# Two-block transformer kernel on one core: the RWKV projections in another order, with a third of the weight splits on GpSimd

## The reference, cut to what matters

```python
x = x + rmsnorm(e, g[5])                    # end of PLE
h = rms_norm(x, g_mix[layer])
h_prev = jnp.pad(h, ((0, 0), (1, 0), (0, 0)))[:, :-1]
hh = h_prev - h
xr, xw, xk, xv, xa, xg = (h + hh * mu[i] for i in range(6))
r = xr @ w_r
w = -softplus(-(w0 + tanh(xw @ w1) @ w2)) - 0.5
k = xk @ w_k
v = xv @ w_v
a = sigmoid(a0 + (xa @ a1) @ a2)
g = sigmoid(xg @ g1) @ g2
kk = k * k_k ; kk = kk / max(norm(kk per head), 1e-12)
k = k * (1 + (a - 1) * k_a)
decay = exp(-exp(w))
# then, for each token: state = state * decay + (state @ -kk) (kk * a)^T + v k^T ; y = state @ r
y = groupnorm(y) + sum(r * k * r_k) * v
x = x + (y * g) @ w_o
```

## Time and profile before

| | |
|---|---|
| median of 3 runs | 1519.14 us (1517.55 to 1521.77) |
| the profiled execution's own time | 1517.85 us |
| its span from first to last instruction | 1516.1 us |
| busy: PE, DVE, ACT, POOL | 94%, 61%, 48%, 10% of the span |
| granted TensorE clock, mean | 0.967 of full speed |
| memory read | 228.51 MB, 151 GB/s over the span |
| PE busy from 678.0 to 821.6 us, the stretch that is changed | 123.31 us of 143.60 |
| DVE, ACT, POOL busy in the same stretch | 114.55, 71.95, 19.80 us |

### The profile page before, as it was taken

How to read it: one execution, slowest core, us unless ns; L and a number is a source line. 1 busy time by engine, 2 the same in 40 slices (tenths; PEclk the granted TensorE clock), 3 DMA queues, 4 the chain that set the end, 5 groups by cost and what they waited for, 6 DMA issues and landing times.

```text
span 1516.1 us, 25989 instructions
## 1 busy us (share of the span) xinstructions
PE 1418.1 (94%) x10670; PEld 1214.2 (80%) x10670; DVE 918.8 (61%) x1257; ACT 724.5 (48%) x976; POOL 147.3 (10%) x138
## 2 busy tenths in 40 slices
PE   8988999998999999988889988899999988799998
PEld 8956888987988999876767766799998865589997
DVE  5665555556576645578877585655555665355563
ACT  5454545446545554454653343354444665254452
POOL 0162011100000110100030011000000123000000
PEclk9999999999999999998998999999999999799999
DMA  8733465564654556544453000365474631245562
GB/s 285 239 92 124 149 207 175 175 192 155 212 165 158 188 188 221 182 154 118 143 177 98 5 3 3 105 216 181 143 244 129 224 110 56 82 163 184 160 214 86
DMA packets 82262, 231.27 MB, mean 153 GB/s; under 512 B 11696, under 2 KB 17472, under 8 KB 82144
## 3 DMA queue, kind: packets, MB, share of 16 engines
q1 hardware_dynamic: 81584, 227.49, 47.0%
q0 software_dynamic: 560, 2.11, 0.4%
HBM read 228.51 MB, written 1.06 MB: 151 GB/s over the span
## 4 chain that ended last, share of the span: by engine, by line
PE 83%; DVE 7%; ACT 4%; issue 3%; POOL 2%; DMA 1%; SPq 0%; DVEq 0%; ACTq 0%; POOLq 0%
PE PS L410 51%; PE PS L413 28%; PE PS L425 4%; ACT SH L382 1%; DVE SL L385 1%; POOL AB L771 1%; DVE XI L1284 1%; DVE AB L745 1%; DVE SL L388 1%; DMA ST<-in_w_attn_in 0%; POOL SM L839 0%; ACT AB L755 0%; DVE LG L1572 0%; DMA ST<-in_w_conv_in 0%; DVE MG L1581 0%
## 5 line engine op out<-in xcount | busy, mean ns | idle before, releaser
L388 DVE SCALAR_TENSOR_TENSOR SL<-ST,SM,SH 128x1024 fp32r<-128x1024 f32 (+1 forms) x256 | 314.8, 1249 | 179.8 <-ACT SH L382 138.5
L382 ACT ACTIVATE SH<-ST,SM 128x1024 fp32r<-128x1024 f32 (+1 forms) x256 | 282.3, 1122 | 215.1 <-PE PS L413 137.9
L410 PE MATMUL PS<-XH,SH 128*128 128x256 f32 x1256 | 353.2, 281 | 5.2 <-DVE XL L1289 3.3
L413 PE MATMUL PS<-XH,SL 128*128 128x256 f32 x1256 | 353.4, 281 | 0.0
L410 PE MATMUL PS<-XL,SH 128*128 128x256 f32 x1256 | 352.4, 281 | 0.0
L385 DVE TENSOR_TENSOR SL<-ST,SH 128x1024 fp32r<-128x1024 f32 (+1 forms) x167 | 216.9, 1315 | 155.1 <-ACT SH L382 131.3
L410 PE MATMUL PS<-SH,XH 128*128 128x512 f32 x576 | 241.3, 419 | 24.0 <-DVE XL L1773 7.5
L382 ACT ACTIVATE SH<-ST 128x1024 fp32r<-128x1024 f32 (+1 forms) x167 | 172.1, 1047 | 181.2 <-PE PS L413 150.4
L410 PEld LDWEIGHTS PS<-XH,SH 128*128 128x128 f32 x1256 | 237.4, 189 | 6.9 <-ACT SH L382 5.7
L410 PEld LDWEIGHTS PS<-XL,SH 128*128 128x128 f32 x1256 | 235.1, 187 | 1.0
L413 PEld LDWEIGHTS PS<-XH,SL 128*128 128x128 f32 x1256 | 235.2, 187 | 0.2
(11 more groups left out here) (310 smaller groups left out, 1433.3 us busy)
## 6 DMA issues: line engine op xcount, KB each, us to landing
ST<-in_ffn_w_gu SPq DMA_DIRECT2D x80, 512.0 KB, 4.8
ST<-in_w_mlp_up SPq DMA_DIRECT2D x64, 512.0 KB, 4.7
ST<-in_w_mlp_down SPq DMA_DIRECT2D x64, 512.0 KB, 4.4
ST<-in_ffn_w_down SPq DMA_DIRECT2D x44, 512.0 KB, 4.4
ST<-in_w_attn_in SPq DMA_DIRECT2D x24, 512.0 KB, 5.0
ST<-in_w_conv_in SPq DMA_DIRECT2D x24, 512.0 KB, 4.6
ST<-in_w_ple_gate SPq DMA_DIRECT2D x16, 512.0 KB, 4.1
ST<-in_kv_w SPq DMA_DIRECT2D x16, 512.0 KB, 4.2
```

The source lines that it names most:

```text
L382: a = ac.do(lambda e: e.activation(h[p0:p1, 0:cols], t[p0:p1, 0:cols], ACT.Copy, scale=sc), ready, t_gt, pe_done.get(i - NSPLIT))
L388: b = ve.do(lambda e: e.scalar_tensor_tensor(l[p0:p1, 0:cols], t[p0:p1, 0:cols], sc, h[p0:p1, 0:cols].bitcast(F32), ALU.mult, ALU.subtract ...
L410: pe.go(lambda e: e.matmul(o, l, r, start=start, stop=stop, skip_group_check=skip))
L413: return pe.do(lambda e: e.matmul(o, l, r, start=start, stop=stop, skip_group_check=skip))
```

## The change

**Units.** The list becomes: K 0 to 7, w1 alone (512 columns), R 0 to 3, a1 (written twice side by side, so that its result lands in partitions 64 to 127), w2 and a2, R 4 to 7, V 0 to 3, g1 (2 units), V 4 and 5, g2 (2 units), V 6 and 7, w_o. PE follows this order. The low part of the odd units of K, R and V and of all eight of w_o is subtracted on POOL.

**The start.** `ple`'s chain becomes a generator with two stops, and half of L1168 moves to POOL (in both layers). The work from `X` to `HT` goes by token halves and feature halves: squares of one half, `X` times gain (DVE), and a float32 matmul of that with a diagonal matrix of the row scales, which transposes and scales at once. HH and the first mix (K's) are made in quarters, two of its low parts on POOL. The first four K units run for the first 128 tokens, then for the others. Two `keep_busy(3, 0)` take the place of `keep_busy(8, 4)`.

**The mixes.** The low parts of mixes 0 (R), 4 (a) and 5 (g) move to POOL, where that of 3 (V) was.

**The decays.** `PX` is exp(0.6065 SG) on ACT times `PP` on POOL, in place of the exclusive sum. The 16 small matmuls and the copy of `PE_` go. Two transfers from SP write 4 rows of `PP` to memory, and four bring them back transposed, 4 bytes at a time. The norm of kk is made in two halves, so the power on POOL becomes two of 16 columns. Buffers of the lanes move accordingly.

```diff
-    for k in range(8):
-        u(rows(A["rw_w_k_2"][0], k, 0, 1024))
-    units.append(("wa1", 0, 128, 1024))
+    eight("rw_w_k_2", range(8), (1, 3, 5, 7))
+    special("w1", 512)
+    eight("rw_w_r_2", range(4), (1, 3))
+    special("a1", 1024)
+    special("wa2", 1024)
+    eight("rw_w_r_2", range(4, 8), (5, 7))
+    eight("rw_w_v_2", range(4), (1, 3))
     for k in range(2):
         u(g1v[:, 4 * k:4 * k + 4, :], 640)
+    eight("rw_w_v_2", range(4, 6), (5,))
     u(A["rw_g2_2"][0][0:128, :])
     u(A["rw_g2_2"][0][128:160, :], p0=96, p1=128)
+    eight("rw_w_v_2", range(6, 8), (7,))
+    eight("rw_w_o_2", range(8), range(8))
...
-            b = ve.do(lambda e: e.tensor_tensor(l[p0:p1, 0:cols], t[p0:p1, 0:cols], h[p0:p1, 0:cols].bitcast(F32), ALU.subtract),
+            b = (po if i in on_pool else ve).do(lambda e: e.tensor_tensor(l[p0:p1, 0:cols], t[p0:p1, 0:cols], h[p0:p1, 0:cols].bitcast(F32), ALU.subtract),
...
-                vs.append(ve.do(lambda e, n=n: e.tensor_tensor(xs_[n], ee[n], g[:, n * 512:n * 512 + 512], ALU.mult), es[n], gt, xn_free[m]))
+            yield
+                vs.append((po if n else ve).do(lambda e, n=n: e.tensor_tensor(xs_[n], ee[n], g[:, n * 512:n * 512 + 512], ALU.mult), es[n], gt, xn_free[m]))
...
+    for _ in rw_steps(0):
+        pass
+    shift_chain(0)
+    second = rw_steps(1)
+    next(second)
+    keep_busy(3, 0)
+    shift_half(0)
+    next(second)
+    mix_part(2, 0, 0, 0, ve)
+    next(second, None)
+    shift_chain(1)
+    keep_busy(3, 0)
+    us = take_group(EDGE, EDGE - 1)
+    k_half(0, range(3))
+    shift_half(1)
+    k_half(0, range(3, 4))
+    mix_part(2, 0, 0, 1, ve)
     for m in range(2):
+        mix_part(2, 0, 1, m, po)
+    k_half(1, range(4))
...
+    kind_a(XM[0], range(4, 5), (0, 1, 2, 3), first=False, last=False)
+    m1 = mix(1, 1)
+    kind_a(XM[0], range(5, 7), (0, 1, 2, 3), first=False, last=False)
+    m0 = mix(0, 2, po)
+    tk = kind_a(XM[0], range(7, 8), (0, 1, 2, 3), first=False)
+    t1, lfw = low_rank_in(4, XM[1], 0, ACT.Tanh, xend, jk_free[0])
+    m4 = mix(4, 0, po)
+    pe.wait(m0)
+    kind_a(XM[2], range(1), (0, 1, 2, 3), last=False)
+    m5 = mix(5, 1, po)
+    pe.wait(m4)
+    t2, lfa = low_rank_in(5, XM[0], 64, ACT.Copy, xend, jk_free[0])
+    m3 = mix(3, 0, po)
...
-    t = cumsum(C_SUI)
-    t_px = ac.do(lambda e: e.activation(PX[:, :, :], ps2, ACT.Exp, scale=-EM05), t, xfree[1])
-    for p in range(8):
-        for m in range(2):
-            t = mm_t(bank(0, p * 4 + 2 * m, p * 4 + 2 * m + 2), PP[:, m, p * 128:p * 128 + 128], CC[:, 63:128:64], True, True)
-    t_pe = ve.do(lambda e: e.tensor_copy(PE_, bank(0, 0, 32)), t)
+    t_ex = ac.do(lambda e: e.activation(PX[:, :, :], SG[:, :, :], ACT.Exp, scale=EM05), t_sg, trr)
+    t_pe = [dma_once(scr2[2 * m:2 * m + 2, :], PP[63:128:64, m, :], t_pp) for m in range(2)]
+    t_b = po.do(lambda e: e.tensor_tensor(AG[:, :, :], AG[:, :, :], KK[:, :, :], ALU.mult), t_kk, a)
+    t_px = po.do(lambda e: e.tensor_tensor(PX[:, :, :], PX[:, :, :], PP[:, :, :], ALU.mult), t_ex, t_pp)
+    t_pe = [dma_once(PE_[:, 8 * mc:8 * mc + 8], scr2[mc, :].rearrange("(p f) -> f p", f=128), t_pe, slow=True) for mc in range(4)]
```

More of the change, by code:

```diff
@@ L1152, in ple, with steps @@
         hr_last = hr_free[0]
-        def chain(m):
+        def steps(m):
             g, gt, gi = pp
@@ L1270, in emit @@
[L1270 to L1275, removed]
+    rw_steps, te1 = ple(1, before, 0)
+    HT = ar("HT", 8, [128, 8, S + 1])
+    HH = ar("HH", 11, [128, 8, S])
+    XI = ar("XI", 13, [128, 8, S])
@@ L1299, in emit @@
     GL2 = ar("GL2", 4, [128, 1, S], F32R, 7168)
[L1300 to L1308, removed]
+    RN, KK, KN = ar("RN", 5, [128, 2, D]), ar("KK", 6, [128, 2, D]), ar("KN", 12, [128, 2, D])
+    TS, SG, AG = ar("TS", 7, [128, 2, D]), ar("SGR", 7, [128, 2, D]), ar("AGR", 8, [128, 2, D])
@@ new lines, in emit @@
+    m3 = mix(3, 0, po)
+    for n, k in enumerate((4, 5)):
+        j, h4, l4 = take(4 - n)
+        for m in range(2):
+            for n2 in range(2):
+                t = mm3(bank(2 * m + n2), [x[:, k, m * 128:(m + 1) * 128] for x in XM[2]], [x[:, n2 * 512:(n2 + 1) * 512] for x in (h4, l4)], False, False)
+        pe_done[j] = t
+    t, _, t_ag = low_rank_out(slice(64, 128), (h, l), AG, pa0, lfa, m3[4], m5[4])
+    pe_done[i] = t
+    trr = kind_a(XM[2], range(6, 8), (0, 1, 2, 3), first=False)
@@ new lines, in emit @@
+    for b4 in range(4):
+        bfree[4 + b4] = t_pi
+    scr2 = nc.dram_tensor("scr2", (4, D), F32).ap()
+    t_pe = [dma_once(scr2[2 * m:2 * m + 2, :], PP[63:128:64, m, :], t_pp) for m in range(2)]
+    kap, kat, kai = param()
+    wait_banks([0, 1, 2, 3])
+    pe.wait(m3)
+    kind_a(XM[0], range(1), (0, 1, 2, 3), last=False)
+    a = [ve.do(lambda e, m=m: e.scalar_tensor_tensor(TT[:, m, :], AG[:, m, :], 1.0, kap[:, :], ALU.subtract, ALU.mult), t_ag, kat, trr) for m in range(2)]
+    par_done(kai, a[1])
@@ L1351, in emit @@
         c = ve.do(lambda e, o=o, hh_=hh_, ll_=ll_: e.tensor_tensor(ll_[:, 0, :], LF[:, o, :], hh_[:, 0, :].bitcast(F32), ALU.subtract), b, xend)
[L1352 to L1362, removed]
+        gsp.append([b, c])
+    a = [ve.do(lambda e, m=m: e.tensor_tensor(TT[:, m, :], TT[:, m, :], rkp[:, :], ALU.mult), a, rkt) for m in range(2)]
@@ new lines, in emit @@
+    par_done(rki, a[1])
+    kind_a(XM[0], range(4, 5), (0, 1, 2, 3), first=False, last=False)
+    ta_ = ve.do(lambda e: e.scalar_tensor_tensor(KK[:, :, :], KK[:, :, :], -1.0, PX[:, :, :], ALU.mult, ALU.mult), t_px, t_b)
+    kind_a(XM[0], range(5, 6), (0, 1, 2, 3), first=False, last=False)
+    wait_banks([4, 5, 6, 7])
+    (i, h, l), (i2, h2, l2) = take_group(2)
+    pe.wait(split_tok[i], split_tok[i2])
+    tt = [None, None]
+    for z2, (src, kp, hl_) in enumerate((((GH, GL), (0, 128), (h, l)), ((GH2, GL2), (96, 128), (h2, l2)))):
+        pe.wait(gsp[z2])
```

336 lines of the change are left out of this document (172 added, 164 removed).

## The result

The changed kernel takes **1536.96 us** in the median of four runs (1534.30 to 1539.71), the kernel before 1518.35 beside it (1516.47 to 1521.77): a ratio of **1.012 [1.0094, 1.0146]**, 18.6 us slower. The prediction said 1522 with a range of 1504 to 1534. It leaned to the right side and missed the size. The profiled execution took 1539.71 us, 2.75 over its median, with a span of 1537.9; the prediction for it was 1520.8, so the miss is 18.9.

A forecast was written before the change was run, and what follows sets the result against it. PE bounds the kernel, DVE sets the pace after K; after the change the port DVE and POOL share decides. 3.4 + 1 - 2 + 0.5 = +2.9 us on 1517.85 gives 1520.8, against medians 1522; range 1504 to 1534.

The forecast's parts named there:

- The port: DVE and POOL instructions streaming two big SBUF tiles exclude each other; from 678 us to the scan's inputs, 107 us becomes 139.
- Where the head lands: Start of the scan: 677.9 + 8 idle + 134.3 to 139.1, plus a 2 us gap; taken as 825, 3.4 later.
- With no gap afterwards: After 8 us idle at the start, the resource shared by DVE and POOL stays full until the scan's inputs are ready.
- PE's side: Rival, 29 in 100: POOL's help costs nothing, PE's 105 us plus waits set the scan's start at 803 to 815; 1507.
- The ledger: From 678 us to the scan's inputs: two-SBUF-operand work of DVE 75.7 and POOL 58.6, 134.3 us, or 139.1 with two w_o splits.
- The early start of K is hidden: K's first units begin at some 688, but K 7's low part waits on DVE, so K ends about 720, as before.
- PE's work: Last gate matmul to the scan: PE's work falls from 115.9 to 105.0 us, 10.9 less, if operands are ready.
- The early scan, +1: The scan's first steps meet the last w_o splits on POOL; between nothing and +2.4 us, taken as +1.
- After the scan, -2: Second half of w_o: three splits leave DVE, but POOL's splits meet DVE's norm steps; -3.5 to +4.8 us, taken as -2.
- two of them in the way: Upper bound behind the scan, +4.8 us: two of POOL's three w_o splits hold up DVE's norm steps.
- The first PLE, +0.5: Half of L1168 on POOL holds up the power behind it, 1.2 us for 0.68, so +0.5.
- POOL is starved: Rival, 19 in 100: in the V stage DVE's block delays PX and V 5; scan starts 829 to 831, about 1530 us.

## Why the prediction was wrong, by its own steps

**The port.** Right, and shown by runs: reads cost 15.1 us where nobody wants the result and writes 4.4; reads taken out of the changed kernel's splits give 15.6 back. I counted in the trace when at least one of the two engines was in an instruction with two SBUF operands. From the last gate matmul to the head of the scan that is 138.9 us after the change and 107.2 before; the prediction had 139 and 107. Part of the agreement is luck. When the scan's inputs were ready, at 831.8, the count stood at 134.5 with two w_o splits and part of a third in it, where the prediction had 139.1 with two; the rest are w_o splits behind it. The Trainium skill, "SBUF — State Buffer", "Who interferes with whom", has POOL's reads as the harmful ones and not its writes; the runs with reads and with writes agree.

**Where the head lands: the step that failed.** The sum was 677.9 + 8 + 139.1, at most 2 more, with the head standing where the port is done. (The sum is 825.0; the 825.3 of the prediction is a slip of no weight.) Two things in it were wrong. The first is the idle time of the port. Until the last input of the scan the trace has 678.9 + 18.4 idle + 134.5 = 831.8, so the idle time was 18.4 us and not 8 to 10. It was not the start in halves: until 720 the port is idle for 9.6 us, and for 9.5 in the kernel before, close to the 8 that were allowed. The excess lies behind 720, 8.8 us, of which 1.3 at 749.1, 2.2 at 769.0 and 4.5 at 785.9, where DVE copies RN out of PSUM and then waits for ACT. "With no gap afterwards" was assumed, not read. The second is the path: the head was not where the port was done, but 4.8 us later, where PE was done. A low part late by DVE's blocked products held PE up, and the prediction costed PE's side only in another case. Together they put the head at 836.7, past the 831 that the prediction itself named as a sign of being wrong.

The ledger was not a chain either. Counted from the last gate matmul, with the splits back on DVE the port works 15.0 us less (123.9) and the head comes 8.7 sooner; with idle reads in the kernel before it works 22.2 more and the head comes 10.4 later. A microsecond of port costs about half a microsecond here, and the rest fills or opens gaps.

**The miss in its parts.** Of the 18.9 us, 10.6 lie in this stretch (14.0 for the 3.4 forecast), 6.2 behind the scan, 0.5 ahead of the stretch and 3.5 in the rest, mostly this execution's distance to its median; the early scan gave 1.9 back.

**"The early start of K is hidden", costed at nothing.** Half right: K's first matmul stands at 688.48, before 690 as forecast, and K ends at 721.3, no sooner. But it is not free. It costs 6.6 and 7.1 us in two pairs of kernels (7.0 and 5.3 by the ratios), of which the traces have 1.4 and 4.9 before the head. What it consists of (DVE's shorter instructions, 0.35 for 128 columns where 256 take 0.48; three waits of PE inside K) I did not separate.

**PE's work.** 105.0 us at full clock was the forecast and 119.23 the reading, at a mean clock of 0.87; a fall of 10.9 was forecast and one of 4.1 came. (The "2 of 10 idle products" in that sum should read 4; its 3.6 us are right for 4.) The reordering was costed at nothing beyond waits, and by subtraction it has a price. Old start, one sum and the transfer, all on DVE, take 1516.00 in the new order and 1510.50 in the old one: 5.5 us, though that pair also differs in the halved kk norm and in buffers. Part of it may be the port again, as the AG product on POOL cost 3.7 us in the new order and nothing in the old one. In the new order PE waits 4.23 us at R's first unit and 8.18 ahead of w2's product, also with nothing new on POOL. My reading, not tested, is that there is less work between K and them to cover the mixes and the tanh. The stretch of that kernel, as a whole:

```profile
676.90:822.10 145.20, 117.31 (x472) 90.06 (x473) 120.19 (x139) 73.04 (x81) 20.14 (x8) 0.86 0.44 136
```

PE works 6.0 us less than before and is idle for 7.6 more: the waits took more than the smaller sums saved.

**The early scan, +1.** The trace has -0.9 to w_o's first group. **After the scan, -2** with bounds -3.5 and +4.8: the trace has +4.2, at the upper bound. The bound of "two of them in the way" is what happened: POOL's three splits meet the norm steps. POOL's row, then DVE's:

```profile
961.82 7.97 POOL L399 TENSOR_TENSOR SL<-ST,SH 128x1024 fp32r<-128x1024 f32 x3
```

```profile
961.89 2.89 DVE L1812 TENSOR_TENSOR RN<-RN,SM 128x512 f32<-128x512 f32 x1 [0.91 <-POOL SM L1810]
964.70 5.64 DVE L1814 TENSOR_TENSOR RN<-RN,PR 128x512 f32<-128x512 f32 x2
970.26 1.28 DVE L1816 TENSOR_TENSOR RN<-RN,PR 128x512 f32<-128x512 f32 x2
```

Two norm products take 5.64 together; the next pair, of the same shape and with POOL done, takes 1.28. **The first PLE, +0.5**: half of its product is 1.67 us on POOL; the stretch ahead grew by 1.0, too little to tell.

**The rivals.** PE ended last, but not as the rival had it, with free operands and a faster kernel: it was idle for 38.5 us. "POOL is starved" had the right place and the wrong victim: V 5 was to wait over 10 us and waited 1.72. Its low part was ready at 810.10 where the rival said 813. DVE did not run its block and lock POOL out; they took turns, DVE came out of three products 10.9 us behind (17.7 for 6.8), and PE paid at GL, 7.34 us, which no case had. A rival that asked what stands behind DVE's blocked products, and not only what stands in POOL's queue, would have found it.

**The sum of it**, in medians: POOL's part 14.4 us (splits 11.3; the products and the mixes are each within the scatter), the new start 6.6, the new order about 5.5 by subtraction; against them one sum, -6.4, and the transfer, -0.6, which is nothing. Together 19.5. That this is near the 18.6 measured proves nothing: the kernels form a chain from one to the other, so the steps must add up, whatever each one's cause.

## What to carry to other kernels

Before work is moved from DVE to POOL, add up both engines' instructions with two SBUF operands as one resource, and then look for what is queued behind each instruction that will now wait. A step taken off the path is only worth it if the next engine has its result sooner: here 5.7 us of matmuls turned into 5.0 us of waiting for a product, and moving another product behind that one brought the head 2.2 us forward. Ask as well which engine ends last: the port's work was forecast well, and PE, held up by one small operand, set the head. Test the parts of a large change alone: 7 us of this one were a gain, hidden by 26.5 of loss.

## What the runs showed of the hardware

POOL waits for DVE's port and DVE for POOL's, and who comes next differs. In the kernel before, POOL's instruction at 755.03 did not get in between two DVE products; the second is recorded from 755.37, 0.08 before the first was over (two took 2.35 us from 754.23). In the changed kernel, TT and the second KN began 0.03 and 0.04 us after the product before them, on whose operands they depend, and POOL got in each time. That the overlap is what keeps POOL out is my reading and was not tested.

Small reads block as large ones do: POOL products of 208 columns, 1.1 us each in the mean and 0.62 at the least, were enough for 15 us, with four at each of twelve units. Not all reads do. POOL's powers of 128x32 read SBUF too, and beside one of 6.37 us, from 770.91 in the kernel before, three DVE splits took 1.22 to 1.23 us. Memsets on POOL next to DVE products cost these nothing (2.29, 1.22, 2.35 us). The four transfers of 4-byte pieces, 4096 in all beside the weight stream, landed 3.0 us after their issue in the median (in the kernel before with one sum and the transfer; size in KB, then us), and no wait in the trace names them:

```profile
SM<-scr SPq DMA_DIRECT2D x4, 4.0 KB, 3.0
```
